# Compression stage: cache pages read where they land, two accumulators per pass instead of turned copies

## What is computed

```python
def _compress(kv_rows, pe_k, w1_k, w2_k, pe_v, w1_v, w2_v, k_norm_g):
    n_cmp = (T - CMP_BLK) // CMP_STRIDE + 1            # 63 blocks of 32 tokens, one each 16
    idx = jnp.arange(n_cmp)[:, None] * CMP_STRIDE + jnp.arange(CMP_BLK)[None, :]
    blk = kv_rows[:, idx]
    def phi(x, pe, w1, w2):
        x = (x + pe[:, None, :]).transpose(0, 1, 3, 2, 4).reshape(B, n_cmp, NSA_GROUPS, CMP_BLK * HEAD_DIM)
        return jax.nn.gelu(x @ w1) @ w2
    kc = _rms(phi(blk[:, :, :, 0], pe_k, w1_k, w2_k), k_norm_g)
    vc = phi(blk[:, :, :, 1], pe_v, w1_v, w2_v)
```

## Time and profile before

| | us |
|---|---|
| median of 3 runs | 2603.04 |
| lowest, highest | 2602.44, 2603.98 |
| profiled execution, its span | 2603.8 |
| PE busy in it | 2531.7 (97%) |
| DVE, ACT, POOL busy | 910.1, 642.8, 483.8 |
| compression stage, PE's first to last record | 371.96 to 555.6 |
| next stage, PE's first record | 558.82 |

### The profile page before, as it was taken

The page is one execution under the profiler, slowest core; times in us unless marked ns, Lnnn a source line. Parts: engine busy times, 40 slices in busy tenths (PEclk is TensorE's granted clock), DMA queues, the critical chain, the costliest instruction groups (busy, mean ns, idle before and its releaser), DMA issues.

```text
span 2603.8 us, 44997 instructions
## 1 busy us (share of the span) xinstructions
PE 2531.7 (97%) x18404; PEld 2104.0 (81%) x18404; DVE 910.1 (35%) x2519; ACT 642.8 (25%) x1643; POOL 483.8 (19%) x473
## 2 busy tenths in 40 slices
PE   9999989989999999999999999999999999999998
PEld 4555556446666644699999999999999999999996
DVE  2133153227766533334223222223323232323222
ACT  1212132137766523211111111111111111111110
POOL 0000022010000212312223312312313131313131
PEclk9999999989999999999999999999999999999999
DMA  5000065032000552687677887888989999999997
GB/s 211 13 25 21 17 188 116 1 99 94 1 2 17 147 153 92 244 291 265 233 273 245 283 279 279 281 297 283 315 313 303 329 311 332 310 328 310 328 309 268
DMA packets 272765, 534.09 MB, mean 205 GB/s; under 512 B 41743, under 2 KB 83703, under 8 KB 272476
## 3 DMA queue, kind: packets, MB, share of 16 engines
q1 hardware_dynamic: 226892, 474.36, 51.5%
q0 software_dynamic: 33456, 47.92, 8.4%
q10 hardware_dynamic: 12208, 8.89, 1.4%
HBM read 492.75 MB, written 43.48 MB: 206 GB/s over the span
## 4 chain that ended last, share of the span: by engine, by line
PE 61%; DMA 2%; issue 1%; DVE 0%; POOL 0%; ACT 0%; SPq 0%; POOLq 0%; ACTq 0%; DVEq 0%
PE first_out L2403 37%; PE eo L2429 18%; PE eo L2253 2%; PE first_out L2253 2%; DMA cache_rows<-summed_rows 0%; DMA out_xp<-w_up 0%; DMA summed_rows<-window_rows,row_index_cur 0%; PE first_out L2331 0%; PE etp L2277 0%; DMA slot_tokens_gates<-token_gate_s,dest_s 0%; POOL summed_rows L2190 0%; PE erp L2299 0%; SPq L2159 0%; DMA slot_rows<-slot_tokens_gates 0%; PE etp L2390 0%
## 5 line engine op out<-in xcount | busy, mean ns | idle before, releaser
L2403 PE MATMUL first_out<-rg_oret,cache_rows 128*128 128x128 f32 (+19 forms) x4096 | 505.2, 285 | 0.0
L2403 PE MATMUL first_out<-rg_oret,w_up 128*128 128x128 f32 (+19 forms) x4096 | 505.2, 285 | 0.0
L2403 PEld LDWEIGHTS first_out<-rg_oret,cache_rows 128*128 128x128 f32 x4096 | 502.2, 191 | 0.5 <-issue 0.5
L2403 PEld LDWEIGHTS first_out<-rg_oret,w_up 128*128 128x128 f32 x4096 | 502.1, 191 | 0.0
L2429 PE MATMUL eo<-rg_oret,mixT 128*128 128x128 f32 (+19 forms) x3968 | 493.2, 286 | 0.0
L2429 PEld LDWEIGHTS eo<-rg_oret,mixT 128*128 128x128 f32 x3968 | 489.2, 191 | 1.1
L2732 DVE TENSOR_SCALAR window_rows<-first_out,b_up_cur 128x128 f32<-128x128 f32 (+19 forms) x256 | 93.6, 366 | 982.8 <-PE first_out L2403 982.8
L2190 POOL DMA_INDIRECT summed_rows<-window_rows,row_index_cur x149 | 235.2, 1579 | 1044.0 <-ACT window_rows L2509 1008.0
L373 PE MATMUL zp<-w_in,xnT 128*128 128x512 f32 (+3 forms) x816 | 301.7, 525 | 2.1 <-DVE xnT L607 1.1
L2523 ACT ACTIVATE window_rows<-window_rows 128x128 f32<-128x128 f32 (+19 forms) x256 | 82.4, 322 | 852.3 <-DVE window_rows L2732 852.3
L373 PEld LDWEIGHTS zp<-w_in,xnT 128*128 128x128 f32 x816 | 147.2, 191 | 134.9 <-issue 115.9
(11 more groups left out here) (513 smaller groups left out, 2104.6 us busy)
## 6 DMA issues: line engine op xcount, KB each, us to landing
cache_rows<-in_w_up SPq DMA_DIRECT2D x64, 2048.0 KB
w_up<-in_w_up SPq DMA_DIRECT2D x64, 2048.0 KB, 12.9
mixT<-in_w_down SPq DMA_DIRECT2D x64, 2048.0 KB, 12.5
w_in<-in_w_in SPq DMA_DIRECT2D x3, 2048.0 KB, 12.0
x<-in_x_prompt SPq DMA_DIRECT2D x8, 512.0 KB, 3.7
w_up<-in_x_prompt SPq DMA_DIRECT2D x8, 512.0 KB, 3.7
summed_rows<-window_rows SPq DMA_DIRECT2D x8, 512.0 KB, 2.7
h_rows<-h SPq DMA_DIRECT2D x8, 512.0 KB, 3.6
```

What stands on the lines that cost most here:

```text
L2403: mm = nc.tensor.matmul(up[c % 2][:, h, :N], U[c // 4][:, h, kk, w0:w0 + P], hT[:, kk, :N], start=(kk == 0), stop=(kk == KC - 1))
```

## The change

The host gives the compression cache in another layout, `cmp_pages`: a page becomes 128 rows (two tokens of a pair by 64 values) of 256 columns (keys or values, group, phase of the pair in its 16-token step, step in the page). A page is one DMA of 128 rows of 1 KB, straight to the place from which PE reads it. For groups 1 and 2 the turning, its PSUM tiles and its copies are gone; the prompt is still turned.

A matmul of a pass now reads, for one phase and one group, 4 sequences x 8 pages x 8 steps = 256 columns. Since a block spans two 16-token steps and the columns of a step cross page borders, the first eight phases accumulate in one PSUM tile and the last eight in another, 512 columns each. DVE copies the first 63 of each 64 columns of the first tile into `hid` and adds the second tile shifted by one column; ACT's Gelu then works in place in `hid`. A pass is 32 matmuls. The tiles are the pair `acc` and the pair `tp[1]`, `tp[2]` in turn.

Group 2's pages have a home of their own, `second_pages`, in the memory that was `xT`; the small `xT` of the prompt and the operands of the retention step lie in it too, so its loads wait for the prompt's passes, the gates, and the stored state (`second_home_free`). `SEQ` is written anew with each pass as an entry of its own. In `load_pages` and the rest, cut to what the prediction speaks of:

```diff
@@ load_pages
-            h = 64 * (pg % 2)
-            if gi == 1:
-                src = k.i["cache_cmp_kv"][0, bass.ds(page, 1)].rearrange("o (m r) k g d -> (o m) (r k g d)", r=2)
-                eng.dma_start(k.x2_rows[b][h:h + 64, pg // 2], src).then_inc(semaphore[gi], 16)
-                continue
-            src = k.i["cache_cmp_kv"][0, bass.ds(page, 1)].rearrange("o (m r) k g d -> (o m) r (k g) d", r=2)
-            dst = k.x2[b][h:h + 64, pg // 2].rearrange("p a (r d) -> p r a d", r=2)
-            for r in range(2):
-                eng.dma_start(dst[:, r], src[:, r]).then_inc(semaphore[gi], 16)
+            src = k.i["cmp_pages"][bass.ds(page, 1)].rearrange("o p x -> (o p) x")
+            eng.dma_start(k.page_home[gi][b][:, pg], src).then_inc(semaphore[gi], 16)
@@ phase_compress
-    SEQ = [("T", 0, 0), ("T", 0, 1), ("M", 0, 0), ("M", 0, 1), ("T", 1, 0), ("S", 0, 0), ("T", 1, 1), ("N", 0, 0),
-           ("S", 0, 1), ("M", 1, 0), ("T", 2, 0), ("S", 1, 0), ("M", 1, 1), ("T", 2, 1), ("N", 1, 0), ("S", 1, 1),
-           ("M", 2, 0), ("S", 2, 0), ("M", 2, 1), ("N", 2, 0), ("S", 2, 1)]
+    SEQ = [("T", 0, 0), ("T", 0, 1), ("M", 0, 0, 0), ("M", 0, 0, 1), ("M", 0, 1, 0), ("M", 0, 1, 1),
+           ("M", 1, 0, 0), ("M", 1, 0, 1), ("S", 0, 0), ("S", 0, 1), ("M", 1, 1, 0), ("N", 0, 0), ("M", 1, 1, 1), ("S", 1, 0),
+           ("M", 2, 0, 0), ("N", 1, 0), ("M", 2, 0, 1), ("S", 1, 1), ("M", 2, 1, 0), ("S", 2, 0), ("M", 2, 1, 1), ("N", 2, 0), ("S", 2, 1)]
+        columns = [ap.rearrange("p b (q v g r n) -> p v r b g q n", q=PAGES, v=2, g=G, r=8) for ap in (k.first_pages, second[:])]
+        halves = [acc, tp[1:]]
+        def second_home_free(eng):
+            eng.wait_ge(s_m, 4)
+            eng.wait_ge(s_gt, 1)
+            eng.wait_ge(s_out, 32)
@@ sync (POOL and ACT alike; ACT's stands behind its Gelu of ("M", 0, 1, 1))
-            sp.wait_ge(s_t, first_t[1, 1] + nT(1))
+            second_home_free(sp)
             load_pages(k, sp, 2, range(4), SP_PAGES, s_x)
-            sp.wait_ge(s_out, 32)
@@ scalar
+                        act.wait_ge(s_hs, n - 3)
+                        src = out
+                    nc.scalar.activation(out, src, ACT.Gelu_apprx_tanh, bias=bias[:, 2 * kv + hh:2 * kv + hh + 1]).then_inc(s_g, 1)
@@ tensor
+                if op == "M" and gi:
+                    hh = half[0]
+                    n = pass_of[gi, kv, hh]
+                    if kv == 0 and hh == 0:
+                        pe.wait_ge(s_x[gi], 16 * nb * len(SP_PAGES))
+                        pe.wait_ge(s_xo[gi], 16 * nb * len(POOL_PAGES))
+                        pe.wait_ge(s_xa[gi], 16 * nb * len(ACT_PAGES))
+                    if n == 4:
+                        pe.wait_ge(s_g, 4)
+                    elif n == 5:
+                        pe.wait_ge(s_rc, 1)
+                    else:
+                        pe.wait_ge(s_hs, n - 5)
+                    for jj in range(16):
+                        out = halves[n % 2][jj // 8]
+                        out = out[:].rearrange("p a b -> p (a b)") if n % 2 else out[:]
+                        out = out.rearrange("p (b g q n) -> p g b q n", b=nb, g=G, q=PAGES)
+                        for g in range(G):
+                            mm = nc.tensor.matmul(out[:, g], w1[kv][jj][:, hh * P:hh * P + P], columns[gi - 1][:, kv, jj % 8, :, g],
+                                                  start=jj % 8 == 0 and g == 0, stop=jj % 8 == 7 and g == G - 1)
+                        if jj == 7:
+                            mm.then_inc(s_h1, 1)
+                    mm.then_inc(s_m, 1)
@@ vector
+            def sum_of_halves(gi, kv, hh):
+                n = pass_of[gi, kv, hh]
+                first, next_ = ((t[:].rearrange("p a b -> p (a b)") if n % 2 else t[:]).rearrange("p (x n) -> p x n", n=64) for t in halves[n % 2])
+                out = hid[:, kv, hh, :].rearrange("p (x n) -> p x n", n=NCMP)
+                dve.wait_ge((s_k, s_v)[kv], gi)
+                dve.wait_ge(s_h1, n - 3)
+                nc.vector.tensor_copy(out, first[:, :, 0:NCMP]).then_inc(s_hc, 1)
+                dve.wait_ge(s_m, n + 1)
+                dve.wait_ge(s_hc, n - 3)
+                nc.vector.tensor_tensor(out, next_[:, :, 1:64], out, ALU.add).then_inc(s_hs, 1)
-                if (op, gi, kv) == ("M", 2, 0):
+                if (op, gi, kv, half) == ("M", 2, 0, [1]):
                     normalise()
@@ kernel
+    rows = given.pop("cache_cmp_kv")[0].reshape(-1, 8, 8, 2, 2, G, HD)
+    given["cmp_pages"] = _np.ascontiguousarray(rows.transpose(0, 3, 6, 4, 5, 2, 1)).reshape(-1, P, 256)
```

More of the change, by code:

```diff
@@ L922, in _ @@
-                    if gi == 0 and kv == 1:
-                        retention()
+                        for e in range(2):
+                            pe.wait_ge(s_te[e], done_by(2 * kv + 2, e))
+                    n = pass_of[gi, kv, hh]
+                    if n >= 2:
+                        pe.wait_ge(s_g, n - 1)
+                    for jj in range(16):
+                        c0 = 64 * (jj % 8) + jj // 8
+                        mm = nc.tensor.matmul(acc[n % 2][:, :126].rearrange("p (g n) -> p g n", n=NCMP),
+                                              w1[kv][jj][:, hh * P:hh * P + P], xT[kv][:, :, c0:c0 + NCMP], start=(jj == 0), stop=(jj == 15))
@@ new lines, in _ @@
+                    mm.then_inc(s_m, 1)
+                    if hh == 0:
+                        pe.wait_ge(s_bp, kv + 1)
+                        for part in range(2):
+                            mm = nc.tensor.matmul(bp[:, HID * kv + part:HID * kv + part + 1], sq_r[:, part * P:part * P + P], share[:],
+                                                  start=True, stop=True)
+                        mm.then_inc(s_b, 1)
+                    if kv == 1 and hh == 1:
+                        retention()
@@ L1029, in _ @@
             nc.vector.memset(share[:], 1.0 / 32)
-            for op, gi, kv in SEQ:
+            for op, gi, kv, *half in SEQ:
                 b0, nb = SRC[gi]
@@ L1046, in _ @@
                         gates()
-                    else:
-                        sample_state()
+                if (op, gi, kv, half) == ("M", 0, 1, [1]):
+                    sample_state()
                 if op == "S" and kv == 0:
```

140 lines of the change are left out of this document (48 added, 92 removed).

## The result

| | before | after |
|---|---|---|
| median, us | 2602.74 (2600.6 to 2603.98, 4 runs) | 2580.96 (2576.52 to 2580.99, 4 runs) |
| span of the profiled execution | 2603.8 | 2579.3 |
| PE, DVE, ACT busy in it | 2531.7, 910.1, 642.8 | 2509.4, 905.7, 625.7 |

The changed kernel takes 0.9909 of the time [0.9895 to 0.9923], 23.7 us less by the ratio and 21.8 by the medians. The forecast was 2584.0 us, 19.0 us less.

What follows compares the result with a forecast made beforehand. TensorE was taken to bound the kernel. Passes 110.72, slots 11.07, clock 1.5, tail 0.21, add and handover 0.73 make 124.23 us against 143.23: 19.0 saved, 2584.0 us forecast; range 2579 to 2589 (0.74), wider 2578 to 2593.

Steps and rivals of the forecast that it cites:

- Which engine sets the end: Compression stage: TensorE runs almost without a gap, so a microsecond saved there is one of the whole.
- The turning and the slots: Compression stage: turning of 25.1 us goes, slots between passes make 11.07 us; 143.23 us to the last Gelu becomes 124.23.
- S(1,0), S(1,1) and S(2,0): Small second-layer matmuls between passes of the compression stage, put at 1.00, 1.98 and 1.00 us.
- The clock term: First new pass: meets the low clock after the retention step, as the first turning did; 1.5 us added.
- The first sum: Ahead of the third pass: PE waits 1.93 us for record 0.45, copy 0.67, add 0.68 and three handovers of about 0.04.
- The passes: Compression stage: each pass is 32 matmuls of 0.4325 us, 13.84 us, 0.27 more than before; eight make 110.72 us.
- The loads: Group 1's pages as 128 rows of 1 KB instead of 64 of 2 KB: shorter rows cost nothing.
- Group 2's loads: Page loads issued after the state store: all land by about 431 us, needed near 469, so nothing on the path.
- Rival 1: Passes: jumps slow the reads; at four columns a jump 27.3 us more, 2611.3 us; chance 0.06, plus 0.04 within 0.2%.
- the PSUM rule: Writes of the passes: Trainium skill says non-contiguous PSUM patterns slow matmuls significantly, no figure; the prediction took no cost.
- Rival 2: Compression stage: saving partly given back as waits, low clock or late pages, 5 to 8 us, 2589 to 2592; chance 0.16.
- Rival 3: Behind the barrier: low-clock stretches come, go or move, 1.5 or 3 us either way, 2581 to 2587; inside the forecast's 0.74.

Runs made afterwards that it cites:

- after_write_contiguous: Changed kernel with accumulators laid out by group first, so each matmul writes 256 neighbouring PSUM columns; 0.9912 of the time of the kernel before.
- after_read_contiguous: Changed kernel with each matmul of groups 1 and 2 reading 256 neighbouring columns instead of runs of eight; 0.9918 of the time of the kernel before.
- after_runs_of_1: Changed kernel with another host layout, so matmuls read single fp32 values 32 bytes apart instead of runs of eight; 1.0403 of the time of the kernel before.

## Why the prediction was right, point by point

- **Which engine sets the end: right.** What PE lost in the stage arrived at its end: from the last Gelu to the next stage it is 7.22 us, 6.94 before, and what runs behind the barrier moved with it.
- **The turning and the slots: right, the total forecast 1.6 us too short.** From the first cache work to the last Gelu 125.82 us against 124.23. S(1,0), S(1,1) and S(2,0) took 1.01, 1.98 and 1.01 us as forecast; a pass with the second mean 16.44 (forecast 16.42), with the first mean 16.02, as this has 63 columns and takes 0.27 us, where 0.62 was taken.
- **The clock term: right in kind, and of a size that a single execution doesn't fix.** The first pass took 16.35 us (406.17 to 422.52) against 13.84 + 1.5, so 1.0 more. The low clock came with the small products of the retention step and lasted from 404.3 to 411.1 us, 6.8 us; 5.0 of them lie in the pass and cost 2.5, and the other 0.9 us are in the retention step (7.69 for 6.79):

```profile
404.00:406.00 2.00, 2.00 (x8) 0.26 (x4) 0.00 (x0) 0.00 (x0) 0.00 (x0) 0.57 0.03 8
406.00:408.00 2.00, 2.00 (x6) 1.51 (x5) 1.41 (x2) 0.00 (x0) 0.00 (x0) 0.50 0.00 0
408.00:410.00 2.00, 2.00 (x6) 1.60 (x5) 0.00 (x0) 0.00 (x0) 0.00 (x0) 0.50 0.83 189
410.00:412.00 2.00, 2.00 (x8) 1.63 (x8) 0.00 (x0) 0.00 (x0) 0.00 (x0) 0.72 0.33 73
```

 The turning had met 3.4 us of low clock, from 408.9 to 412.3. The same pass meets 3.4 us in after_write_contiguous and takes 15.38 us there, as forecast, and in after_read_contiguous it meets none and takes 13.92:

```profile
402.97 11.49 PE L919 MATMUL cacc<-w_in 128*128 128x256 f32 x52
...
416.89 11.39 PE L919 MATMUL ctp<-w_in 128*128 128x256 f32 x52
...
403.00:411.00 8.00, 8.00 (x39) 7.07 (x38) 1.41 (x2) 0.00 (x0) 1.08 (x2) 1.00 0.45 110
```

 So the price of 1.5 us lay in the middle of what this pass meets, 0 to 2.5 us, and a bound of 2.5 was missing.
- **The first sum was mis-sized.** The slot ahead of the third pass is 2.40 us, not 1.93: the add starts 0.46 us after its copy's end, where 0.04 was taken; the same 0.46 us stand in the profiles of all eight kernels of this order. The second sum's add follows its copy in 0.11, and the cause of the difference stays open. The copy at 0.68 and the add at 0.68 were right.
- **The passes** at full clock take 13.90 to 14.01 us, where 13.84 was forecast: 0.217 to 0.219 us a record for 0.2163. Key passes into `ctp` are the shortest; why the others are 0.1 us longer was not looked into.
- **The loads: the step that was wrong.** "I cost the shorter rows at nothing" looked only at whether a page would be late. The same pages also share the DMA engines with the value weights, whose wait, 5.15 us, with its low clock, stood in the earlier trace rows, taken only as evidence on the clock. The 3.1 us that the wait lost and what follows it came to 5.9 us in the profile. By runs it is 0.0022 of the time [0.0011 to 0.0033], 5.7 us, in the kernel before.
- **Group 2's loads: right.** The state store is issued at 407.72, SP's twelve loads end at 424.66 (12.91 us from 411.75), POOL's at 425.6; the pages are needed at 469.81.
- **Rival 1 and the PSUM rule: refuted for the runs and gaps used here**, by contiguous reads and contiguous writes at the same 0.218. The rival would have been right for single values, by far: runs of one made the kernel 4.0% slower than before. The step that ruled it out at runs of eight rested on runs of 32, so on a row four times as long.
- **Rival 2: did not happen between the passes.** PE idled 1.49, 1.67 and 1.82 us, and the clock stayed at 1.00 through all of them:

```profile
413.00:533.00 120.00, 113.25 (x561) 97.08 (x559) 29.83 (x53) 12.48 (x19) 5.91 (x11) 1.00 0.11 35
```

 The fourth, 1.83 us ahead of the last mean, was followed by 0.50 and cost 0.3 us. That the clock holds is not assured: in after_runs_of_1 it fell to 0.50 at 467.2 us, 1.7 us after an idle time of 1.49, and again behind 1.67 and 1.83.

- **Rival 3 (the time behind the barrier) was larger than priced:** -4.9 us, where 1.5 to 3 either way were taken, and 8.4 us lie between the shortest and longest such span of these kernels. No kernel of the changed order has as long a span as any of the order before.
- **The sum of the misses.** -5.9 (loads), -4.9 (behind the barrier), +2.5 (projection), +0.9, +1.6 and +0.3 is -5.5, the difference between the 24.5 us gained between the profiles and the 19.0 forecast. Against the forecast of 2584.0 the median is 3.0 us lower. That it came so near is in part luck: the 17.4 us gained in the turning and passes are the forecast's own, and two terms that it did not have in its sum, 10.8 us together, were halved by 5.3 us of losses that it did not have either.

## What to carry to other kernels

Ask of a changed transfer not only whether its data come in time, but what other load shares the DMA engines in that stretch: every wait for a DMA that a trace shows near it is part of the sum. Here a landing on 64 partitions slowed its neighbours, and a load across all 128 was worth more than the longer row it gave up. When a hand-over to another engine is put behind a pass, place the small work of PE there first, so that its sum or square has a pass of cover; here this order was worth 5.0 us of idle time in the stage, about a fifth of the whole change, though the whole times don't show it clear of their noise. And compare two kernels measured in different sets of runs by their ratios to a third, not by their medians.

## What the runs showed of the hardware that was not expected

- A matmul whose moving operand is read in single fp32 values takes 0.462 us a record of 256 columns, against 0.219 to 0.222 for pairs and 0.218 for eights and one run. The 0.46 us are the same at a granted clock of 0.50 and of 1.00, where a record of the others takes 0.44 and 0.216.
- Writing PSUM in runs of eight fp32 values with gaps costs a matmul nothing measurable: 0.218 us a record.
- Pages landing on 64 partitions held the whole DMA traffic to 238 to 255 GB/s with all engines busy, where 128 gave 332 and 333, and delayed a 512 KB load that had nothing to do with them: it landed after 14.3 to 15.5 us in five profiles, and after 10.5 to 13.0 in the eight with pages on all partitions.
- Waits for the weights of 1.0 to 2.5 us left the clock at 1.00, and those of 3.52 to 6.02 us, like an idle time of 6.30 us, were each followed by 0.50. Idle times of 1.5 to 1.8 us between passes mostly left it at 1.00, but not always: 0.50 followed one of 1.83 us in the changed kernel, and ones of 1.49, 1.67, 1.82 and 1.83 us with single-value reads.
- Kernels with the same code behind a barrier differed by up to 8.4 us in 2040 there, with 13.7 to 37.5 us of low clock, and by up to 3.8 us where the order ahead of the barrier was the same too. From single profiles here, a smaller difference can't be told.
